# Thirty products of constants in six waits of TensorE, in a two-block transformer kernel

## What is computed

```
# first block: one layer
h  = rmsnorm(x, n1) * (1 + sc1) + sh1
q, k, v, gb, gcv, u, ga, gv = split_proj(h @ w_in)
x  = x + g1 * merge_branches(windowed_attention(...) @ w_attn_out, conv_branch(...))
h2 = rmsnorm(x, n2) * (1 + sc2) + sh2
x  = x + g2 * peer(h2, w_q, sub_keys, u_tab, v_tab)
...
# peer: 8 heads, each picks 16 of 16384 experts for each token
s = (t @ w_q) @ sub_keys        # two halves of 128 keys each
idx = the 16 best pairs         # top_k of sums of two top_k
act = gelu(u_tab[idx] . t)
out = sum(softmax(best) * act * v_tab[idx])
...
# second block: two layers
x = x + attention(rmsnorm(x) @ w_qkv) @ w_o
x = x + conv_ffn(rmsnorm(x), w_up, conv_w, conv_b, w_down)
return rmsnorm(x)
```

## Time and profile before

| | |
|---|---|
| runs before | 1580.48 us median of 3 (1579.15 to 1586.56) |
| span of the profiled execution | 1577.9 us |
| TensorE busy with products | 1413.4 us, 90% |
| TensorE loading weights | 1042.8 us, 66% |
| VectorE busy | 1074.8 us, 68% |
| ScalarE busy | 777.4 us, 49% |
| GpSimd busy | 295.1 us, 19% |
| moved by DMA | 432.91 MB, mean 274 GB/s |

### The profile page before, as it was taken

One profiled execution on the slowest core, in us unless ns is written; L12 is line 12 of the kernel. 1 busy time (PEld: TensorE's weight loads), 2 busy tenths in 40 slices (PEclk: granted clock), 3 DMA queues, 4 the chain that ended last, 5 costly groups with the idle time before them and its releaser, 6 DMA issues.

```text
span 1577.9 us, 21891 instructions
## 1 busy us (share of the span) xinstructions
PE 1413.4 (90%) x7816; PEld 1042.8 (66%) x7816; DVE 1074.8 (68%) x2270; ACT 777.4 (49%) x1649; POOL 295.1 (19%) x296
## 2 busy tenths in 40 slices
PE   7999988899998778778778889998999998999998
PEld 3889987544453223223222278998999987989997
DVE  4678665766666667766665578547777775477776
ACT  3655542444444444444444364746555566455555
POOL 0001100444454444434344300000000010000000
PEclk9999998999999999999999999999999999999999
DMA  9456755999999999999999944234555531245553
GB/s 398 177 204 224 249 175 211 372 418 427 427 426 427 427 427 426 427 426 427 427 427 426 428 186 154 106 108 161 183 175 179 182 127 61 94 167 184 188 186 130
DMA packets 62586, 432.91 MB, mean 274 GB/s; under 512 B 7073, under 2 KB 7585, under 8 KB 12193
## 3 DMA queue, kind: packets, MB, share of 16 engines
q0 software_dynamic: 41616, 285.76, 43.7%
q1 hardware_dynamic: 20160, 145.37, 26.0%
q10 hardware_dynamic: 720, 0.62, 0.1%
HBM read 430.67 MB, written 1.05 MB: 274 GB/s over the span
## 4 chain that ended last, share of the span: by engine, by line
PE 61%; DMA 19%; ACT 9%; DVE 8%; issue 2%; POOL 0%; ACTq 0%; DVEq 0%; POOLq 0%
PE banks L668 26%; PE banks L1059 15%; DMA arena<-in_peer_uv,experts 11%; DMA tok_b<-in_peer_uv,experts 4%; PE banks L1227 3%; PE banks L1195 3%; PE banks L705 3%; DVE wlow L1746 3%; ACT diag L1515 2%; PE banks L864 2%; PE banks L905 2%; PE banks L766 1%; ACT whigh L1271 1%; PE banks L824 1%; PE banks L845 1%
## 5 line engine op out<-in xcount | busy, mean ns | idle before, releaser
L1059 PE MATMUL banks<-arena,diag 128*128 128x512 f32 x780 | 382.9, 624 | 84.9 <-ACT diag L1515 84.9
L1746 DVE TENSOR_TENSOR wlow<-wring,whigh 128x1024 fp32r<-128x1024 f32 x234 | 276.0, 1221 | 121.5 <-ACT whigh L1271 121.4
L2190 DVE CUSTOM_DVE_ANT_0 arena<-arena,scores 128x1024 f32<-128x1024 f32 x200 | 245.2, 1226 | 162.5 <-DMA arena<-in_peer_uv,experts 160.5
L1059 PEld LDWEIGHTS banks<-arena,diag 128*128 128x128 f32 x780 | 140.2, 193 | 315.7 <-ACT diag L1515 191.5
L1271 ACT ACTIVATE whigh<-wring 128x1024 fp32r<-128x1024 f32 x234 | 234.6, 1050 | 97.6 <-DMA wring<-in_w_down 34.3
L1695 POOL DMA_INDIRECT arena<-in_peer_uv,experts x200 | 210.5, 1052 | 314.8 <-PE banks L1059 264.6
L668 PE MATMUL banks<-f_high,whigh 128*128 128x256 f32 x720 | 205.2, 285 | 8.0 <-DVE wlow L1746 5.5
L668 PE MATMUL banks<-f_low,whigh 128*128 128x256 f32 x720 | 203.7, 283 | 0.0
L668 PE MATMUL banks<-f_high,wlow 128*128 128x256 f32 x720 | 203.7, 283 | 0.0
L1507 ACT ACTIVATE dots<-dots 128x1 f32<-128x1 f32 x256 | 51.9, 203 | 302.3 <-DVE dots L2190 302.0
L668 PE MATMUL banks<-a_high,whigh 128*128 128x256 f32 x528 | 159.3, 302 | 11.8 <-DVE a_low L1792 6.0
(11 more groups left out here) (275 smaller groups left out, 2411.1 us busy)
## 6 DMA issues: line engine op xcount, KB each, us to landing
wring<-in_w_up SPq DMA_DIRECT2D x44, 1024.0 KB, 4.9
wring<-in_w_down SPq DMA_DIRECT2D x22, 1024.0 KB, 4.9
wring<-in_w_in SPq DMA_DIRECT2D x17, 1024.0 KB, 5.4
wring<-in_w_qkv_a SPq DMA_DIRECT2D x12, 1024.0 KB, 4.9
arena<-in_w_mod SPq DMA_DIRECT2D x8, 1024.0 KB, 15.6
arena<-in_w_mod_t POOLq DMA_DIRECT2D x16, 512.0 KB, 5.3
hT<-in_w_mod_t POOLq DMA_DIRECT2D x16, 512.0 KB, 4.7
wring<-in_peer_w_q SPq DMA_DIRECT2D x5, 1024.0 KB, 4.8
```

Of the source, the lines that this page charges most:

```text
L1059: mm = nc.tensor.matmul(banks[:, 2 + 2 * b + half, :], diag[:, n % DIAGS, :], ring[ROW_PLACE[n]][:, D + half * 512:D + (half + 1) * 512], ...
L1746: V.tensor_tensor(low, w, high.bitcast(F32), ALU.subtract).then_inc(w_split, 1)
L2190: V.tensor_tensor_reduce(out=ring[ROW_PLACE[n]][:, 0:D], in0=ring[ROW_PLACE[n]][:, 0:D], in1=h2tok[:, b, :], scale=1.0, scalar=0.0, op0=AL ...
```

## The change

A helper makes products of `averaging` with the first 256 columns of `const`, both constants, into the lower half of a bank that nobody reads before it is written anew. It is called at six waits of TensorE: two products before the second norm's sum and seven behind it, eight before the first layer's slots, three in the second layer's slot 2, six before the wait for `o_ready` in the first layer (none in the second), and four before the last down projection of the first layer. The first two calls stand about one norm's sum. The wait for `o_ready` moves behind the waits for `roped2` and `proj2_read`. Nothing that is read changes.

```diff
+            def constant_products(count, bank):
+
+                for _ in range(count):
+                    nc.tensor.matmul(banks[:, bank, 0:T], averaging, const[:, 0:T], start=True, stop=True)
+
...
+            constant_products(2, 5)
             norm_sum(x_squares)
             pe.wait_ge(keys_in, 16)
+            constant_products(7, 5)
...
                 plan, chunks2 = plans[1 + l], len(proj2[l])
+                if l == 0:
+                    constant_products(8, 2)
                 for slot in range(plan["slots"]):
                     n, j = divmod(slot, 2)
+                    if l == 1 and slot == 2:
+                        constant_products(3, 6)
                     if n < chunks2:
                         project(n, j)
...
-                        pe.wait_ge(o_ready, 4 + 4 * l)
                         pe.wait_ge(roped2, r)
                         pe.wait_ge(proj2_read, m)
+                        if early == 0:
+                            constant_products((6, 0)[l], 0)
+                        pe.wait_ge(o_ready, 4 + 4 * l)
                         pe.wait_ge(score_read, plan["groups"][-1]["n"] + 1)
                         wo_rows(l, min(early, 1), ((0, 1), (0,), (1,))[early])
...
                 def ffn_down_banks(i):
 
+                    constant_products(4, 6)
                     pe.wait_ge(ff_ready, i + (f0 + 1))
```

## The result

The changed kernel takes 1572.38 us, the median of 20 runs (1567.84 to 1579.14); the kernel before, 20 runs beside them, 1580.67 us (1576.12 to 1586.68). The ratio is 0.9949, with a 95% interval of 0.9937 to 0.9961. Measured once more, beside the last experiments, the ratio was 0.9975 (0.9961 to 0.9988). Both say that it is faster, by 4 to 8 us; the forecast was 9.1 us and a time of 1571.5 us.

The account below looks back on a forecast made before the run. Outside a DMA-bound middle part, TensorE's products were most of the path, slowed by half clock behind waits. Gains 3.2 + 0.7 + 2.3 + 1.5 + 1.4 = 9.1 us gave 1571.5 us, 8-in-10 range 1566 to 1578.

Parts of the forecast that it names:

- The waits: TensorE's waits at the filled places would shrink to about 1.1, 0.5, 0.4, 0.7, 0.4 and 0.1 us.
- The clock: TensorE's granted clock would be 1.00 in all the stretches behind the filled waits, where it stood at 0.50.
- the harmless 1.60 us: A TensorE wait behind which the clock didn't fall; at the second norm, waits left under it were taken as held.
- Second norm and query, 3.2 us: Two and seven products about the second norm's sum: first query 6.91 instead of 10.08 us, first gathered rows equally earlier.
- the rival of the middle part: Gathers held by something not moving with the query turn the 3.2 us into idle DMA time: 1574.6 us; chance 0.10.
- First layer, 0.7 us of 2.7: Eight products before the first layer's queries: TensorE gains 2.7 us, VectorE's addition of squares leaves about 0.7.
- Attention's output, 2.3 us: Six products in the first layer's wait of 3.29 us: 8.10 - 5.75 = 2.3 us gained and kept.
- Down projection and second layer's first query, 1.5 + 1.4 = 2.9 us: Four products in a wait of 2.12 us gain 1.5 us, three in one of 1.36 us gain 1.4 us.
- The rival that short waits fall only sometimes: Waits of 2.12 and 1.36 us may pass at full clock in other executions: 6.2 us gain, 1574.3 us; chance 0.22.
- the 0.5% border: Whole kernel: 7.9 us from no change, at 1572.6 us; faster than that got 0.58.
- The rival of late products: Filled waits don't hold the clock; seven products take 6.0 us in 3.5; 3.5 us lost, 1584.0 us; chance 0.06.

Follow-up runs that it names:

- the seven alone: The changed kernel with only the seven products behind the second norm's sum, without the two before it and the other places; one run, 1580.88 us.
- one-column products: The changed kernel with each of the 30 constant products narrowed from 256 columns to one, their number unchanged; 1579.87 us, ratio 0.9996.
- the version with five more places: The changed kernel with five more waits filled: first projections, first block's output mix, first gathered row, two in second layer's attention; 1564.88 us, ratio 0.9888.

## Why the prediction was right

Step by step, by the traces:

- **The waits.** Predicted 1.1, 0.5, 0.4, 0.7, 0.4 and 0.1 us to be left; measured 0.92, 0.57, 0.41, 0.90 (0.69 in the second trace) and 0.39, and no wait listed at the sixth. The price of 0.43 us for a product held.
- **The clock.** Held at all six, in both traces. With the columns taken out of the products it was held at none. The reason given, that the waits left lie under the harmless 1.60 us, was not a good one: the prediction's own rows have a fall behind 1.36 us. That what was left (up to 1.08 us) would be harmless was not in the rows, and it turned out so.
- **Second norm and query, 3.2 us:** 2.9 (10.08 - 7.16 in the chain; 13.57 - 10.65 in the table). The query itself took 7.16 and not 6.9 us, for it still waits a little for ScalarE's tiles. The first gather came 2.99 us earlier, and the middle part took as long as before to within its scatter: the rival of the middle part fell.
- **First layer, 0.7 us of 2.7:** 0.68 in the pair of traces. The reason was right, but the term was too sure: with the place unfilled it is 0 in two other traces (7.62 and 7.63 us), where a shorter low stretch hides behind VectorE, and 0.9 in the seven alone. Alone it wasn't measurable. On the mean of these four traces the term is 0.4 us.
- **Attention's output, 2.3 us:** 2.07. The other three traces with the place unfilled give 1.4, 2.2 and 2.1.
- **Down projection and second layer's first query, 1.5 + 1.4 = 2.9 us:** 2.80, and 2.6 to 2.8 by the other unfilled traces. The rival that short waits fall only sometimes had 0.22, and was wrong for these two places: in all four traces that left both waits as they were, and in the one with one-column products, the clock was at 0.50 behind both. Its mechanism does exist in this kernel, at the wait of 2.14 us before the first projections, which fell in six traces of twelve; nothing in the prediction's rows told that the two places would be of the other kind. This also answers what the prediction left open, whether a fall can differ from run to run of one kernel: it does. The Trainium skill's limit for idle gaps (TensorE: Matmul & The Clock Gate, "Why this matters for your kernels"), by which these two places would have given nothing, is contradicted by each of these traces: the clock fell behind 2.12 and 1.36 us.

Together 2.9 + 0.7 + 2.1 + 2.8 = 8.5 us by the two profiled executions. The first measurement gives 8.3 us between medians, the second 5.2. The spans of the two profiled executions are 10.1 us apart; the missing 1.6 us is mostly the rest (83.42 - 81.80), where the change does nothing. The sum was thus right to within its terms. What it lacked is the scatter: the times of one kernel spread over 10 us, by the clocks above with low stretches at waits that nobody fills, so that a difference of medians is uncertain by a few microseconds. The first ratio lies on the one side of the 0.5% border on which the forecast put 0.58, the second clearly on the other. That the first median came within 0.9 us of the forecast is in part luck; the second, 1575.54 us, is 4 us above it.

**The rival of late products** had its condition tested by the seven alone, and its price was too high. It said that if the clock is at 0.50 when the seven begin they take 6.0 us and nothing is won. They took 4.4 us and 2.35 us were won, for the clock rose while they ran. In the version with five more places they began at full clock and the fall caught them; that cost 0.87 us of the 2.9.

## What to carry to other kernels

Look for waits of the matmul engine of a microsecond or more that are followed by wide products, and ask for the granted clock behind them: here the fall cost 2.7 to 2.9 us at the query, 1.4 to 2.2 at `w_o` and 2.6 to 2.8 at the two short waits together, beyond their own length. Filling such a wait with products of constants cost nothing as long as they ended before it did, and products beyond that delayed what followed by what they took; count them from the wait's length at the full clock, and leave no second long wait just in front. Then ask what comes next without that stretch, since at the first layer another engine took most or all of the gain. Take more than one trace before and after: an unfilled wait can fall in one execution and not in the next.

## What the runs showed of the hardware

- Weight loads and products of one column did not hold TensorE's clock. It fell from 1.00 to 0.50 at 254.28 us in the midst of 10.24 us of them without a gap, and the low clock outlasted them by 5.4 us of wide products; it fell at 933.53 us in the midst of another 10.90 us. I had not expected a busy engine to lose its clock. In the second layer's attention 13.65 us stayed at 0.50 with TensorE busy all the time. The Trainium skill (TensorE: Matmul & The Clock Gate, "Part 4: PE-mode transpose") says that transposes don't bring the full clock; the 13.65 us have transposes in them among other work, so they don't contradict it, and no run here has transposes alone.
- One-column float32 products are far from free: 28 of them took 10.24 us, mostly at half clock, and seven 1.62 us at full clock, against 0.43 us for one of 256 columns.
- Whether a given short wait brings a fall isn't decided by its length alone. A wait of 1.60 us at the load of `w_up` (1080.99 us in the trace before) (1.59 to 1.61) passed at full clock in all 14 traces, while one of 1.36 us fell in each of the four that left it alone, and one of 1.33 us, before the down projection, in the run with one-column products. One of 2.14 us fell in six traces of twelve, one of them and one of the others being of the same kernel. By what it is decided these runs don't settle; nothing was tried that would move a wait in time without changing anything else.
